# Second expert layer of a two-block model: from two experts at a time in column groups of 64 places to four at a time in column groups of 32

## The reference

```python
def hier_moe(v, w_grp, b_grp, w_exp, b_exp, w_gate, w_up, w_down):
    # v: 256 tokens x 1024
    grp_prob = softmax(vt @ w_grp + b_grp)            # 4 groups
    p_grp, g_sel = top_k(grp_prob, 1)                 # one group per token
    in_grp = (vt @ w_exp + b_exp) of that group       # 8 experts
    p_in, e_sel = top_k(softmax(in_grp), 2)           # two experts per token
    w = p_grp * p_in / sum(p_in)
    for e in range(32):
        hdn = silu(vt @ w_gate[e]) * (vt @ w_up[e])   # 1024 -> 512
        y = y + (combine[:, e:e + 1] * hdn) @ w_down[e]   # 512 -> 1024
```

## Time and profile before

| | |
|---|---|
| median of 3 runs | 2195.0 us (2191.34 to 2196.78) |
| the profiled execution, its own time | 2191.13 us |
| its span, first to last instruction | 2189.4 us |
| mean granted TensorE clock over the span | 0.986 of full |
| read from HBM | 705.29 MB |
| second experts: first gate multiply to last down multiply | 1709.84 to 2177.0 us of the span |

### The profile page before, as it was taken

One profiled execution on the slowest core, in us unless ns is written; L12 is line 12 of the kernel. 1 busy time (PEld: TensorE's weight loads), 2 busy tenths in 40 slices (PEclk: granted clock), 3 DMA queues, 4 the chain that ended last, 5 costly groups with the idle time before them and its releaser, 6 DMA issues. The chain is left out here.

```text
span 2189.4 us, 25314 instructions
## 1 busy us (share of the span) xinstructions
PE 2082.8 (95%) x10244; PEld 1023.4 (47%) x10244; DVE 538.4 (25%) x1147; ACT 367.0 (17%) x628; POOL 98.6 (5%) x185
## 2 busy tenths in 40 slices
PE   6989999989999999999999999899899899999998
PEld 4677676643333333333333333365464444444443
DVE  2255453431211122112112211322353200000001
ACT  2133421210000000000000000213341111111112
POOL 2010052000000000000000000100030000000000
PEclk9999999999999999999999999999999999999999
DMA  9332255559999999999999999834253699999995
GB/s 340 107 125 86 77 197 192 212 237 426 428 429 428 429 428 429 428 428 429 428 429 428 429 428 430 324 116 167 62 205 140 251 427 430 428 429 429 428 429 228
DMA packets 98558, 707.05 MB, mean 323 GB/s; under 512 B 12314, under 2 KB 17932, under 8 KB 61516
## 3 DMA queue, kind: packets, MB, share of 16 engines
q1 hardware_dynamic: 98508, 706.36, 78.5%
HBM read 705.29 MB, written 1.05 MB: 323 GB/s over the span
## 5 line engine op out<-in xcount | busy, mean ns | idle before, releaser
L1645 PE MATMUL ps<-ring,arena 128*64 128x512 f32 x2048 | 449.8, 593 | 24.4 <-DMA ring<-in_moe_w_gu 24.4
L1645 PEld LDWEIGHTS ps<-ring,arena 128*64 128x64 f32 x2048 | 145.6, 137 | 323.1 <-issue 266.3
L2819 PE MATMUL ps<-ring,arena 128*64 128x512 f32 x1024 | 225.3, 593 | 8.2 <-DMA ring<-in_w_up 6.4
L1672 PE MATMUL ps<-ring,arena 128*64 128x512 f32 x1024 | 225.1, 592 | 0.0
L2819 PEld LDWEIGHTS ps<-ring,arena 128*64 128x64 f32 x1024 | 78.8, 137 | 151.4 <-issue 151.4
L1696 ACT ACTIVATE arena<-arena 128x512 f32<-128x512 f32 x32 | 20.2, 630 | 769.6 <-DVE arena L1727 769.6
L1039 PEld LDWEIGHTS ps<-arena 128*128 128x128 f32 x1088 | 128.4, 196 | 41.9 <-issue 38.9
L1672 PEld LDWEIGHTS ps<-ring,arena 128*64 128x64 f32 x1024 | 73.2, 137 | 146.5 <-issue 128.1
L1039 PE MATMUL ps<-arena 128*128 128x128 f32 x1088 | 137.9, 284 | 2.6 <-DVE arena L1031 2.6
L2072 PE MATMUL ps<-ring 128*128 128x512 f32 (+1 forms) x320 | 139.6, 586 | 0.7 <-ACT ring L2451 0.6
L2840 PE MATMUL ps<-ring,arena 128*64 128x512 f32 x512 | 113.4, 595 | 0.0
(11 more groups left out here) (571 smaller groups left out, 1930.4 us busy)
## 6 DMA issues: line engine op xcount, KB each, us to landing
ring<-in_moe_w_gu SPq DMA_DIRECT2D x128, 2048.0 KB, 23.9
ring<-in_moe_w_down SPq DMA_DIRECT2D x64, 2048.0 KB, 21.2
ring<-in_w_down SPq DMA_DIRECT2D x32, 2048.0 KB, 13.3
ring<-in_w_gate SPq DMA_DIRECT2D x32, 2048.0 KB, 14.9
ring<-in_w_up SPq DMA_DIRECT2D x32, 2048.0 KB, 17.2
ring<-in_w_in SPq DMA_DIRECT2D x22, 2048.0 KB, 8.5
ring<-in_ada_w SPq DMA_DIRECT2D x12, 2048.0 KB, 9.4
ring<-in_w_out SPq DMA_DIRECT2D x6, 2048.0 KB, 8.5
```

Source lines behind the costliest of these rows:

```text
L1645: last = M.matmul(ps[halves[j], 4 + which, :], xgT[buf][:, k, CAP * ee:CAP * ee + CAP], w[:, k2, at:at + 512], start=False, stop=(k == KD ...
L1672: last = M.matmul(ps[halves[j], 6, :], yT[:, k % KH, halves[k // KH]], w[:, k % KH, 512 * j:512 * j + 512], start=False, stop=(k == 2 * KH ...
L2819: last = M.matmul(ps[halves[j], 4 + which, :], xgT[:, k, halves[j]], w[j][:, k, :], start=(k == 0), stop=(k == KD - 1))
```

## The change

The second experts are taken four at a time. An item is a quad of experts with twelve chunks (four gate, four up, four down); an expert has 32 places in a pass (`CAP2`), up to eight passes are possible, and a step of `s_done` stands for four chunks. The twelve chunks of an item go through the same six slots, chunk c in slot c % 6. Before a load SP waits for the step in which the slot's former chunk is multiplied. `load_first` still loads six chunks ahead: now four gate chunks and two up chunks.

```diff
+CAP2 = 32
+QUAD = 4
...
         def load_rest(self, sp, items):
-            n = sp.value_load(passes[0:1, 0:1], min_val=1, max_val=MAXP)
+            n = sp.value_load(passes[0:1, 0:1], min_val=1, max_val=self.most)
+
+            for c, (src, k, w) in enumerate(self.chunks(0)):
+                if c >= SLOTS:
+                    sp.wait_ge(self.s_done, (c - SLOTS) // self.per_done + 1)
+                    sp.dma_start(slot(c % SLOTS, k, w), src).then_inc(self.full[c % SLOTS], 16)
 
             def load(item, base):
-                for s, (src, k, w) in enumerate(self.chunks(item)):
-                    sp.wait_ge(self.s_done, base * self.steps + s // self.per_done + 1)
-                    sp.dma_start(slot(s, k, w), src).then_inc(self.full[s], 16)
+                for c, (src, k, w) in enumerate(self.chunks(item)):
+                    sp.wait_ge(self.s_done, base * self.steps + (c + self.count - SLOTS) // self.per_done + 1)
+                    sp.dma_start(slot(c % SLOTS, k, w), src).then_inc(self.full[c % SLOTS], 16)
...
-    loads2 = ExpertLoads("experts2", gate_up_down2, 2)
+    loads2 = ExpertLoads("experts2", gate_up_down2, 3 * QUAD, QUAD, MAXP2)
+    quads = [slice(CAP2 * e, CAP2 * (e + 1)) for e in range(QUAD)]
```

On TensorE the two-way loops become four-way, in the gate and up steps and in the down step alike:

```diff
-                            w = [loads.arrived(pe, 2 * which + j, i) for j in range(2)]
+                            w = [loads.arrived(pe, QUAD * which + e, i) for e in range(QUAD)]
                             for k in range(KD):
-                                for j in range(2):
-                                    last = M.matmul(ps[halves[j], 4 + which, :], xgT[:, k, halves[j]], w[j][:, k, :],
+                                for e in range(QUAD):
+                                    last = M.matmul(ps[quads[e], 4 + which, :], xgT[:, k, quads[e]], w[e][:, k, :],
                                                     start=(k == 0), stop=(k == KD - 1))
                             last.then_inc(s_done, 1)
```

Gather, transposes and scatter keep their size, and there are eight items in a pass in place of 16. The one-hot matrix is made by one VectorE instruction, from `iota_all`, a row of the numbers 0 to 255 that GpSimd writes at the start of the second mixer. `later_tables` is no longer called for this layer. The weighted matrix is the product of the one-hot matrix and the weights:

```diff
+    def quad_onehot(onehot, slots, first, ready):
+        V.tensor_tensor(onehot.rearrange("p t (e c) -> p t e c", e=QUAD), rep(rep(first, QUAD), T), bcast(slots, CAP2),
+                        ALU.is_equal).then_inc(ready, 1)
...
+            G.iota(iota_all, pattern=[[1, T * P]], base=0, channel_multiplier=0,
+                   allow_small_or_imprecise_dtypes=True).then_inc(s_iota2, 1)
...
-            pool.wait_ge(s_m11, 2)
-            later_tables(pool, s_gat2, s_slot2)
...
+            vv(V.tensor_copy(gate_of2[:, :, NE:NI2], gate_of2[:, :, 0:QUAD]))
+            vv(V.tensor_scalar(slot_of2[:, :, NE:NI2], slot_of2[:, :, 0:QUAD], -float(CAP2), None, ALU.add))
+            pass_count(4, CAP2)
...
-                        make_onehot(onehot, any_slot_of, i + 1, s_one)
-                        for t in range(T):
-                            for j in range(2):
-                                ins = V.tensor_scalar(gated[:, t, halves[j]], iota_row[:, 0, :], slot_of[:, t, bass.ds(i * 2 + j, 1)],
-                                                      gate_of[:, t, bass.ds(i * 2 + j, 1)], ALU.is_equal, ALU.mult)
-                        ins.then_inc(s_gat, 1)
+                        dve.wait_ge(s_one, i + 1)
+                        V.tensor_tensor(gated.rearrange("p t (e c) -> p t e c", e=QUAD),
+                                        onehot.rearrange("p t (e c) -> p t e c", e=QUAD),
+                                        bcast(gate_of2[:, :, bass.ds(q * QUAD, QUAD)], CAP2), ALU.mult).then_inc(s_gat, 1)
+                        dve.wait_ge(s_gat, i + 1)
+                        quad_onehot(onehot, slot_of2[:, :, bass.ds(q * QUAD + QUAD, QUAD)], iota_all[:, bass.ds(p * CAP2, CAP2)], s_one)
```

More of the change, by code:

```diff
@@ L878, in program @@
     iota_row = sb("iota_row", [P, 2, CAP])
+    MAXP2 = T * P // CAP2
+    NI2 = NE + QUAD
+    slot_of2, gate_of2 = ar(13600, T, NI2), ar(13600 + T * NI2, T, NI2)
+    iota_all = masks[:, 0:T, :].rearrange("p a b -> p (a b)")
     passes = sb("passes", [1, 1], I32)
@@ L911, in first_slots, with pass_count @@
         dve.wait_ge(s_slot, 1)
-        vv(V.tensor_scalar(slot_of[:, :, 0:NE], tmp2, -1.0, None, ALU.add))
-    def pass_count(rank_bank):
+        vv(V.tensor_scalar(table[:, :, 0:NE], tmp2, -1.0, None, ALU.add))
+    def pass_count(rank_bank, cap):
         vv(V.tensor_reduce(cmax[:, 0:1], ps[:, rank_bank, 64:96], X_AXIS, ALU.max))
-        vv(V.tensor_scalar(cmax[:, 1:2], cmax[:, 0:1], float(CAP), 1.0, ALU.is_gt, ALU.add))
-        for b in range(2, MAXP):
-            vv(V.scalar_tensor_tensor(cmax[:, 1:2], cmax[:, 0:1], float(b * CAP), cmax[:, 1:2], ALU.is_gt, ALU.add))
+        vv(V.tensor_scalar(cmax[:, 1:2], cmax[:, 0:1], float(cap), 1.0, ALU.is_gt, ALU.add))
+        for b in range(2, T * P // cap):
+            vv(V.scalar_tensor_tensor(cmax[:, 1:2], cmax[:, 0:1], float(b * cap), cmax[:, 1:2], ALU.is_gt, ALU.add))
         vv(V.tensor_copy(passes[0:1, 0:1], cmax[0:1, 1:2]))
@@ L962, in program, with __init__ @@
     class ExpertLoads:
-        def __init__(self, name, chunks, per_done):
-            self.name, self.chunks, self.per_done = name, chunks, per_done
-            self.steps = SLOTS // per_done
+        def __init__(self, name, chunks, count, per_done, most):
+            self.name, self.chunks, self.count, self.per_done, self.most = name, chunks, count, per_done, most
+            self.steps = count // per_done
+            self.rounds = count // SLOTS
             self.full = [sem(f"{name}_slot{s}_full") for s in range(SLOTS)]
@@ L997, in load_rest, with arrived @@
             return n
-        def arrived(self, pe, s, i, k=KD, w=512):
-            pe.wait_ge(self.full[s], i * 16 + 16)
-            return slot(s, k, w)
+        def arrived(self, pe, c, i, k=KD, w=512):
+            pe.wait_ge(self.full[c % SLOTS], i * (16 * self.rounds) + 16 * (c // SLOTS + 1))
+            return slot(c % SLOTS, k, w)
     halves = [slice(CAP * j, CAP * (j + 1)) for j in range(2)]
@@ L1983, in gate_up_down2 @@
     def gate_up_down2(q):
[L1985 to L1988, removed]
-    loads2 = ExpertLoads("experts2", gate_up_down2, 2)
+        quad = [QUAD * q + e for e in range(QUAD)]
+        return ([(one(w_gt, e).rearrange("(p k) n -> p k n", k=KD), KD, 512) for e in quad]
+                + [(one(w_up, e).rearrange("(p k) n -> p k n", k=KD), KD, 512) for e in quad]
+                + [(one(w_d2, e).rearrange("(p k) n -> p k n", k=4), 4, 1024) for e in quad])
+    loads2 = ExpertLoads("experts2", gate_up_down2, 3 * QUAD, QUAD, MAXP2)
[3 more added lines that the diff above has]
+                        ALU.is_equal).then_inc(ready, 1)
     FIRST = 6
@@ L2769, in program, with expert_quads @@
     s_p13 = sem("final_weight_loaded")
-    def expert_pairs(loads, x_tok):
+    def expert_quads(loads, x_tok):
         KH = 4
-        NP = NE // 2
+        NQ = NE // QUAD
         xgT, sg, y, yT = ar(7168, KD, P), ar(8192, 512), ar(8704, KH, P), ar(9216, KH, P)
@@ L2792, in _ @@
                 sp.dma_start(gfin, row_everywhere(a["g_final_2"])).then_inc(s_p13, 16)
-                loads.load_rest(sp, NP)
+                loads.load_rest(sp, NQ)
             @block.tensor
@@ L2807, in scatter @@
                                      skip_group_check=True)
-                n = pe.value_load(passes[0:1, 0:1], min_val=1, max_val=MAXP)
+                n = pe.value_load(passes[0:1, 0:1], min_val=1, max_val=MAXP2)
                 with pe.Fori(0, n) as p:
-                    with pe.Fori(0, NP) as q:
-                        i = p * NP + q
+                    with pe.Fori(0, NQ) as q:
+                        i = p * NQ + q
                         pe.wait_ge(s_xgt, i + 1)
@@ L2834, in _ @@
                         last.then_inc(s_GT, 1)
-                        w = [loads.arrived(pe, 4 + j, i, 4, 1024) for j in range(2)]
+                        w = [loads.arrived(pe, 2 * QUAD + e, i, 4, 1024) for e in range(QUAD)]
                         pe.wait_ge(s_yTt, i + 1)
@@ L2838, in _ @@
                             for k in range(KH):
-                                for j in range(2):
-                                    last = M.matmul(ps[halves[j], (4, 7)[d], :], yT[:, k, halves[j]],
-                                                    w[j][:, k, 512 * d:512 * (d + 1)], start=(k == 0), stop=(k == KH - 1))
+                                for e in range(QUAD):
+                                    last = M.matmul(ps[quads[e], (4, 7)[d], :], yT[:, k, quads[e]],
+                                                    w[e][:, k, 512 * d:512 * (d + 1)], start=(k == 0), stop=(k == KH - 1))
                             if d == 0:
@@ L2856, in _ @@
                 take_gathered(0)
-                n = act.value_load(passes[0:1, 0:1], min_val=1, max_val=MAXP)
+                n = act.value_load(passes[0:1, 0:1], min_val=1, max_val=MAXP2)
                 with act.Fori(0, n) as p:
-                    with act.Fori(0, NP) as q:
-                        i = p * NP + q
```

(2 more changed lines are left out.)

37 lines of the change are left out of this document (18 added, 19 removed).

## The result

The changed kernel takes 2236.55 us (median of 4 runs, 2234.59 to 2241.56) against 2193.75 before (4 runs, 2191.34 to 2196.78): ratio 1.0196, 95% interval 1.0181 to 1.021, so 2.0% slower. Forecast were 2241 us and a range of 2190 to 2270. The profiled execution has a span of 2232.3 us, where the sum gave 2235.3.

A forecast was written before the change was run, and what follows sets the result against it. The DMA was taken to bound the kernel. From the first multiply, 20.0 + 22 steps at 22.0 + 9.1 + 12.4 = 525.5 us against 479.6, so 2195.0 + 45.9 = 2241 us, 2.1% slower; range 2190 to 2270.

The forecast's parts named there:

- What binds: Second experts' stage before the change: DMA binds at 29.36 us a pair, TensorE 2.4% behind.
- One pass: Second experts: largest list 29 tokens, under 32, so one pass; two passes would give about 2770 us, chance 0.01.
- the multiplies: Second experts: a quad's step of 64 records takes 6.9 to 7.1 us at full clock, as two chunks did before.
- The loads and the clock: Second experts: 0.1 + 7.2 + 2.0 (clock) + 7.8 + 4.9 = 22.0 us a step, 2.4 us over the stream's pace.
- start to issue: Each quad step: start to the load issue its end releases, 7.2 us, plus 2.0 us of clock loss.
- issue to landing: Load of chunk 2 of the next step, nothing in the queue: 7.8 us, with 10.0 us kept for the range.
- landing to start: Each quad step: from the last chunk's landing to the step's start, 0.1 us.
- The waits: TensorE in the second experts: some 12 us before each gate and up step, some 4.9 us before a down step.
- The DMA share: Second experts' stage after the change: share about 0.89, about 380 GB/s.
- the rival in which the clock holds: Second experts: queue runs dry only slightly, steps of 20.0 us, no difference, 2195 us; chance 0.10.
- a dear restart: Second experts' loads: landings take 10.0 us each time, step 24.2 us, 2291 us; chance 0.08 together with an all-half-clock case.
- Start, end, small edits: Stage's ends: first step 20.0 us, last multiply 9.1, tail 12.4; small edits counted as 0, first multiply staying at 1709.84.

The follow-up runs named there:

- e5: The kernel before (pairs of experts, 64 places) with two added slots of 2 MB in free SBUF: 2184.57 us, ratio 0.9967 to the kernel before.
- e2: The changed kernel with eight slots instead of six, the two added ones in free SBUF: 2183.5 us, ratio 0.996 to the kernel before.
- e6: The changed kernel with idle matmuls (14, 5 and 15) while TensorE would wait: 2225.85 us, ratio 1.0147 to the kernel before.
- e1: The changed kernel with fewer idle matmuls (12, 4 and 12) while TensorE would wait: 2231.89 us, ratio 1.0158 to the kernel before.
- e3: The changed kernel with chunks holding half of the row blocks of two experts, six slots: 2184.48 us, ratio 0.997 to the kernel before.

## Why the prediction was right

**What binds.** That the DMA bound the settled pairs, with TensorE 2.4% behind, is borne out by e5: with two more slots and nothing else changed TensorE never waits for a load, and a pair takes its 28.6 us. Where TensorE's work is about halved and the stream is kept running (e2), the rate is the same 429 GB/s.

**One pass** and **the multiplies** held: 1536 records; a quad's step at full clock took 7.08 us.

**The loads and the clock.** The forecast step was 22.0 us and it is 21.89. The parts, means over the 22 steps: start to issue 9.3 us, 9.2 forecast; issue to landing 7.5 us, 7.8 forecast; chunk 3 another 4.9; landing to start 0.2, 0.1 forecast. The errors are small and partly cancel. The waits are 12.5 to 12.9 us ahead of gate and up steps (some 12 forecast) and 4.7 to 5.0 ahead of down steps (4.9). The DMA share in the two stretches is 0.92 and 0.93 and not 0.89, the GB/s 379 and 388 (some 380 forecast).

**A split that was not right.** I priced the clock at the full 2.0 us by which it lengthens a step and so gave the rival in which the clock holds a step of 20.0 us and no loss. e6 measured it: 20.96 us. The term "issue to landing, 7.8 us" was taken as a constant. On average it is 7.5 us when the issue comes 9.3 us after the step's start, and 8.6 us when it comes after 7.4. So by e6 the clock alone is worth 0.9 us a step, and 1.4 us are lost to the look-ahead of two slots at full clock; look-ahead alone, at a fallen clock, takes back all 2.3 (e2). The sum was right because its terms were those of the state in which the chain then ran: rows 6 show a load issued with nothing in the queue, and the slow multiplies bring the issue to about that point. Priced at full clock, the same terms gave 20.0 us a step, 1 us too little. Rows 7 had the other case, a load issued 2.1 us before the landing ahead of it, which took 10.0 us; the prediction kept it as a dear restart and didn't tie it to the early issue.

The page "TensorE: Matmul & The Clock Gate" of the Trainium skill, in its part on HAM oscillation, has each burst start throttled after a wait for data; the trace agrees for every step but the first. These steps are longer than the page's bursts and got the full clock back on the way: 8.3 to 10.1 us, far from the 14.1 us of a wholly slow one. To keep TensorE from idling, which the page's remedies aim at by other means, is what e6 does, and it won back less than half.

**Start, end, small edits.** First step 19.62 us (20.0), last 8.77 (9.1), tail 12.4 (12.4). The one-hot matrix took 0.43 us in place of 0.74, and the gather started 0.2 us sooner. In both kernels the granted clock was 0.50 until about 1706.1, so the gather ended only 0.1 us sooner (1707.88), and the first multiply stayed where it was.

Open is why a load that is issued 2 to 4 us before the landing ahead of it often leaves a gap in the stream, of anything up to 3 us. The runs bound it (0.75 us a step at a release after 6 us, none with four chunks ahead) and don't explain it.

## What to carry to other kernels

When several loads are needed at once and their slots are freed at once, count what is left in front of the DMA engines while they are used: two transfers of six slots here, in place of four. That number must cover the multiplies, at the clock they will have after a wait, and the time by which the next load must be issued ahead (about 5.5 us here). A grouping that halves the work of an engine which is not the bound can still cost time by the granularity in which it takes and returns buffers; cut the chunks across the group, or add slots, and the cost is gone.

## What the runs showed of the hardware

- An idle gap of 2.0 us ahead of a step, in a stage where TensorE was otherwise busy (e1), was followed by a granted clock of 0.50 in the step's first part (8.77 us in place of 7.07). It isn't so each time: in e6 steps after gaps of 2.0, 2.1 and 2.9 us ran at full clock (7.07 us), and steps after 2.3 and 2.5 us did not (8.77). The shortest gap ahead of a fallen clock of which I had a row was 6.45 us.
- Loads issued earlier into a running queue landed later after their issue (9.2, 8.6, 8.0 and 7.5 us on average for issues 6.1, 7.4, 8.5 and 9.3 us into a step), so that a shorter multiply gives back only about half of itself. Issued 5.5 to 10 us ahead of the landing before it, a load of 2 MB followed it in 5.0 us or less (194 of 196).
- Pieces of 8 KB in a row move at 422 GB/s (e3), of 16 KB at 429 (e2).
